# Seven weight slots in the last expert stage, with the residual copied to DRAM and back

## What is computed

```python
def ec_moe(h, router_w, w1, w3, w2):
    affinity = jax.nn.softmax((h @ router_w).astype(jnp.float32), axis=-1)
    gate, idx = lax.top_k(jnp.swapaxes(affinity, 1, 2), cap)      # cap = 32 tokens for each of 16 experts
    xg = jax.vmap(lambda hb, ib: hb[ib])(h, idx)
    hid = jax.nn.silu(jnp.einsum('becd,edf->becf', xg, w1)) * jnp.einsum('becd,edf->becf', xg, w3)
    out = jnp.einsum('becf,efd->becd', hid, w2) * gate[..., None].astype(h.dtype)
    return jax.vmap(lambda ob, ib: jnp.zeros((n, d), ob.dtype).at[ib.reshape(-1)].add(ob.reshape(-1, d)))(out, idx)

def channel_sublayer(x, mod, ng, router_w, w1, w3, w2):
    h = modulate(rmsnorm(x, ng[2]), mod[3], mod[4])
    return x + mod[5] * rmsnorm(ec_moe(h, router_w, w1, w3, w2), ng[3])
```

## Time and profile before

| what | value |
|---|---|
| median of 3 runs | 2848.91 us (2847.16 to 2852.49) |
| the profiled execution, its own time | 2851.62 us |
| its span in the profile | 2849.9 us |
| what lies around the span | 1.7 us |
| PE busy | 2375.7 us (83%) |
| DVE, ACT, POOL busy | 800.5, 525.7, 323.1 us |
| data moved | 707.61 MB, mean 248 GB/s |

### The profile page before, as it was taken

How to read it: one execution, slowest core, us unless ns; L and a number is a source line. 1 busy time by engine, 2 the same in 40 slices (tenths; PEclk the granted TensorE clock), 3 DMA queues, 4 the chain that set the end, 5 groups by cost and what they waited for, 6 DMA issues and landing times. The chain is left out here.

```text
span 2849.9 us, 41403 instructions
## 1 busy us (share of the span) xinstructions
PE 2375.7 (83%) x18056; PEld 1190.5 (42%) x18056; DVE 800.5 (28%) x1636; ACT 525.7 (18%) x1106; POOL 323.1 (11%) x483
## 2 busy tenths in 40 slices
PE   4999998479789888888959968999986988788887
PEld 1333445354344333333324446888873322222222
DVE  2002617380231111111143025676632110101001
ACT  1000212770210000000030024444411000000001
POOL 0000000350100000000032006353410000000000
PEclk8999999689899999999979978999988999999999
DMA  7765210212299999999942234223226999999997
GB/s 275 251 237 193 71 52 30 71 51 96 81 404 425 425 424 424 425 425 424 425 163 66 69 136 75 53 48 69 40 51 258 424 425 425 425 424 425 425 425 294
DMA packets 203348, 707.61 MB, mean 248 GB/s; under 512 B 90404, under 2 KB 125964, under 8 KB 149280
## 3 DMA queue, kind: packets, MB, share of 16 engines
q1 hardware_dynamic: 202240, 704.57, 63.0%
q10 hardware_dynamic: 928, 0.39, 0.1%
HBM read 688.68 MB, written 16.20 MB: 247 GB/s over the span
## 5 line engine op out<-in xcount | busy, mean ns | idle before, releaser
L1593 PE MATMUL bank<-moe_w,moe_xT 128*32 128x512 f32 (+3 forms) x2760 | 576.3, 568 | 148.8 <-DMA moe_w<-in_exp_w 148.2
L1593 PEld LDWEIGHTS bank<-moe_w,moe_xT 128*32 128x32 f32 (+1 forms) x2760 | 177.1, 123 | 546.7 <-issue 371.2
L1620 PE MATMUL bank<-moe_w,moe_hidT 128*32 128x512 f32 (+1 forms) x1276 | 294.4, 594 | 14.4 <-ACT moe_hidT L1661 10.2
L1691 DVE TENSOR_TENSOR moe_silu<-bank,moe_silu 64x512 f32<-64x512 f32 (+3 forms) x96 | 61.8, 644 | 709.1 <-ACT moe_silu L1654 709.1
L1654 ACT ACTIVATE moe_silu<-bank 64x512 f32<-64x512 f32 (+3 forms) x96 | 53.1, 554 | 998.4 <-PE bank L1593 998.4
L1620 PEld LDWEIGHTS bank<-moe_w,moe_hidT 128*32 128x32 f32 (+1 forms) x1276 | 94.7, 122 | 189.6 <-issue 174.3
L1735 POOL TENSOR_TENSOR moe_xn<-moe_xn,moe_w 128x1024 f32<-128x1024 f32 x6 | 18.1, 3016 | 1351.9 <-ACT moe_w L1670 1351.9
L1704 DVE COPY moe_rows<-bank 32x512 f32<-32x512 f32 x96 | 65.8, 686 | 372.0 <-PE bank L1620 371.1
L467 PE MATMUL bank<-w_slab,mixT 128*128 128x512 f32 x384 | 166.4, 593 | 1.5 <-PE bank L467 1.5
L1855 PE MATMUL bank<-mixture,rw_slab 128*128 128x512 f32 (+1 forms) x384 | 143.6, 527 | 4.6 <-PE bank L1855 3.7
L464 PE MATMUL bank<-mixT,w_slab 128*128 128x512 f32 x320 | 142.6, 599 | 1.7 <-PEq L292 1.7
(11 more groups left out here) (486 smaller groups left out, 3076.4 us busy)
## 6 DMA issues: line engine op xcount, KB each, us to landing
moe_w<-in_exp_w SPq DMA_DIRECT2D x346, 1408.0 KB, 28.8
x_res<-in_exp_w SPq DMA_DIRECT2D x38, 1408.0 KB, 25.1
conv_out<-in_ada_w SPq DMA_DIRECT2D x24, 1536.0 KB, 6.4
w_slab<-in_ab_w_in SPq DMA_DIRECT2D x11, 2048.0 KB, 9.1
ada_slab<-in_ada_w SPq DMA_DIRECT2D x8, 1536.0 KB, 12.5
mixT<-ss_rows SPq DMA_DIRECT2D x32, 256.0 KB, 3.2
wo_slab<-in_ab_w_out SPq DMA_DIRECT2D x16, 512.0 KB, 3.5
x_inv_and_t<-x_blocks SPq DMA_DIRECT2D x32, 256.0 KB
```

The costliest lines, as they stand in the source:

```text
L1593: mm = pe.matmul(g.ps[k][64 * m:64 * m + M, 0:hi - lo], xg[:, i % 2, j, c, :], w[:, (2 * m + r) * FF + lo:(2 * m + r) * FF + hi], start=(c ...
L1620: mm = pe.matmul(g.ps[5 + m][64 * m:64 * m + M, :], hidt[:, c, :], w[:, at:at + 512], start=(c == 0), stop=(c == FC - 1))
L1691: ins = dve.tensor_tensor(hid[:, lo:hi], g.ps[k][64:64 + M, 0:hi - lo], hid[:, lo:hi], ALU.mult)
```

## The change

```diff
--- before.py
+++ after.py
@@ -1315,8 +1315,8 @@
     NB = NE // 4
     SL = [(0, 512), (512, 1024), (1024, FF)]
     UNITS, PER = 6 * NE, 6
-    NS = 6 if t0 else 5
-    spill = not t0
+    NS = 7 if t0 else 5
+    spill = True
     XSLOT = (UNITS - NS) % NS
     first = segs[0]
     w1, w3, w2 = (a[n][layer] for n in ("exp_w1", "exp_w3", "exp_w2"))
```

## The result

20 runs of each version: before 2851.25 us (2847.16 to 2856.84), after 2857.12 us (2853.23 to 2861.54). The ratio of the runs is 1.0021, 95% interval 1.0014 to 1.0028: slower by 5.9 us (4 to 8). Forecast: 6.3.

The account below looks back on a forecast made before the run. Bound: a weight stream at 425 GB/s whose last landing plus a fixed tail sets the end. Terms 4.93 + 1.05 + 0.3 = 6.3 us on the median 2848.91 gave 2855.2 us, range 2851.5 to 2858.5.

Parts of the forecast that it names:

- The bound: Last stage: a full weight stream at 425 GB/s, its end the last landing plus a fixed 35.5 us tail.
- The seventh slot: Last stage's weight ring: one more slot gains 0, as six already keep the DMA engines fed.
- Rival 2: Last stage's stream: the extra slot lets engines run ahead, returning 2 to 4 us of the copy; 2852 us, chance 0.13.
- The copy out: Store of x to DRAM at the last stage's start: 4.93 us transfer plus 1.05 dip, 5.98 us.
- Rival 3: Copy out hidden beside the loads, so not slower: 2847 to 2849 us, chance 0.07.
- The wait and the barrier: Last stage's start: SP's wait for the copy holds the barrier, PE's first gather 21 us later, alone costing nothing.
- The dry queue: Before unit 7 at the last stage's start: a short margin costs 0 to 1.1 us, taken as 0.3.
- the margin: Time left in the queue when unit 7 is issued: between 0.4 and 3.3 us, middle 1.9 us taken.
- Rival 1: Queue empties before unit 7 because release or gather is later than reckoned: 8 to 10 us, 2858 us, chance 0.10.
- PE's cold start: PE's first gather in the last stage: starts cold before and after alike, cost 0.
- The copy back: Load of x at the last stage's end, behind unit 95: delays no weights, cost 0, bounds 0 and 4.9 us.
- rival 4: Tail waits up to 4.9 us for the load of x back or the gain rows: 2860 us, chance 0.02.

Follow-up runs that it names:

- e9: Kernel before, six slots, no copy, with router weights and units 0 to 5 issued in the output projection stage ahead: 2844.45 us, ratio 0.9976.
- e3: Changed kernel's seven slots without the copy out; input x loaded at the end instead: stage 680.41 us, ratio to before 0.9993.
- e8: Kernel before with five slots in the last stage in place of six, no copy: stage 680.07 us, ratio 0.9997.
- e2: Kernel before, six slots, plus the copy of x to DRAM behind unit 4, not copied back: stage 686.63 us, ratio 1.0020.
- e1: The changed kernel run once more, unaltered: stage 688.29 us, ratio to before 1.0027.
- e4: Changed kernel with SP's wait for the copy and issue of unit 5 moved behind the barrier: stage 687.10 us, ratio to before 1.0018.
- e7: Changed kernel with only the latents' two token tiles copied out and back, 1024 KB for 2048: stage 684.67 us, ratio to before 1.0017.
- e6: Changed kernel with the copy issued behind unit 6 instead of unit 4: stage 691.98 us, ratio to before 1.0040.
- e5: Changed kernel with the copy issued ahead of unit 0 instead of behind unit 4: stage 686.07 us, ratio to before 1.0018.

## Why the prediction was right, and where it was off

- **The bound** (a landing plus a fixed tail, the queue full). Right: e9 moved the end by moving the stream, and up to DVE's last addition the tail is 31.2 us in both kernels. The store behind it grew by 0.35 us, which stands in no term; "if the tail grows" was a sign of being wrong.
- **The seventh slot, 0.** Right: e3 -0.2 us, e8 -0.5 with one fewer. Rival 2, that part comes back, falls with e3.
- **The copy out, 5.98.** Right in size, by other parts: e2 has 6.03, of which 0.4 are the last store and 5.6 ahead of the last landing. The dip reckoned at 1.05 is 0.3 to 0.5 us ahead of the copy in after, e1, e2, e4 and e7; e6 has none, and in e5 only 0.2 us are lost. So 5.3 us of e2 are transfer and dip, and some 0.3 ahead of the landing are open, as is the cause of the dip. Rival 3 (a hidden store) falls with e2.
- **The wait and the barrier.** Right in mechanism: SP holds the barrier, the gather comes 21.6 us late (21 reckoned), unit 7 is issued 10.4 us behind the release (10.3 reckoned). The release came 44.1 us after the first weight issue and not 43.0, though the dip was 0.5 us smaller than reckoned. Start-up and landing of the copy together were thus 44.11 - 39.04 (16.59 MB at 425 GB/s) - 0.54 = 4.5 us, where the prediction took 2.9 from the first stage.
- **The dry queue, 0.3.** This term was mis-sized: the runs showed 1.2 (e1 less e4), 1.4 by the windows of the changed kernel, 1.9 by those of e1. "If the queue stands idle for over 1 us" was a sign of being wrong, and it came. The step that failed is the margin, taken in the middle of 0.4 to 3.3 us and found nil. Counting back 13.6 us from the queue's end at 2220.2, the copy was through at about 2206.6, and SP was released 3.1 us later, more than the 2.9 I had for start-up and landing together. e6 shows 1.8 for a release with nothing behind it; why it is longer with a unit queued behind is open (an engine that lags behind the others would do it, and was not tried). The Trainium skill (DMA: Bandwidth & Descriptors, section Anatomy of one DMA), which the prediction sets beside this margin, gives its 2 us for DMAs issued by GpSimd; they would have left 1.3 us, the measured 3.1 leave nearly none. Rival 1 named the mechanism but asked for 8 to 10 us. PE's catching up was right: it waits for no weights until three experts on (2330 us), then again for landings.
- **PE's cold start, 0.** Right: the granted clock at the gather's start is 0.50, 1.2 GHz, before and after, and the gather's first row takes 3.54 and 3.75 us (3.75 in e2 with PE on time).
- **The copy back, 0.** Right: rival 4 falls with the tail. e4 less e2 is 0.5 us for slot and copy back together; as the two tails are equal, it lies ahead of the last landing and is not the copy back's. Its cause is open.

From e2, e4 and e1 the stage splits into 6.0 + 0.5 + 1.2 = 7.7 us (differences of one chain, so they add up by construction), against 6.3. By the windows it is 4.93 of transfer, 0.5 of dip, 1.4 of dry queue, 0.35 in the last store and 0.35 open. That the first result, 5.9, came out so near to the forecast is in part luck: the dip was taken 0.5 us too large, the dry queue 1.1 too small, and 0.7 us had no term. The interval of 4 to 8 us holds both 6.3 and the stage's 7.6.

## What to carry to other kernels

Where one DMA queue is full from a stage's start to its last landing, further buffers gave nothing (five, six and seven slots within 0.5 us), and bytes put ahead of that landing cost at least their transfer time (5.1 us ahead of it with the copy first, 5.6 behind unit 4, for 4.93). A wait on a landing must not stand ahead of a barrier that others need; put it behind. Look for the time in which the queue is idle, here the stage before: starting the stream there paid 7 us, and after that a further slot some 6 by the profiles, once the barrier was free of its wait.

## What was not expected of the hardware

A 2048 KB store in a stream of loads put the last landing off by 5.6 us (e2) and 5.1 (e5), the bytes alone at 425 GB/s being 4.9. The rate dipped beside it in five of six kernels. Ahead of the copy that cost 0.3 to 0.5 us; at its end, in e5, it fell by 40% for 2 us, but a burst of 479 GB/s at the start had made up for most of that. Every kernel with the copy, also those that copied half of it, ended 0.4 us later behind its last addition. An issue into an empty queue brought data after about 1.5 us (e6), and one at the moment the queue ended still lost 1.4. SP got word of the copy's landing 1.8 us after the rate fell in e6, and about 3.1 us after the copy's reckoned end with a unit queued behind it.
